# Sparse attention: index weights projected with tokens moving, and the last block's index sum on GpSimd

## What is computed

```python
h = x @ w_in
c_q, c_kv, k_idx, w_idx = jnp.split(h, [Q_LORA, Q_LORA + KV_LORA, Q_LORA + KV_LORA + IDX_DIM], axis=-1)
c_q = rms_norm_2(c_q, q_norm_g)             # 256 wide
c_kv = rms_norm_2(c_kv, kv_norm_g)          # 128 wide, "the latent"
q_idx = (c_q @ w_qidx).reshape(B, S, IDX_HEADS, IDX_DIM)
k_idx = layer_norm(k_idx, kidx_g, kidx_b)
w_idx = w_idx * (IDX_HEADS ** -0.5 * IDX_DIM ** -0.5)   # 8 weights per token
...
    s_idx = jnp.einsum('bthd,bsd->bths', qi_b, k_idx)
    score = jnp.einsum('bths,bth->bts', jax.nn.relu(s_idx), wi_b)
    score = jnp.where(causal[None], score, -jnp.inf)
    _, sel = lax.top_k(score, topk)         # topk = 128
```

## Time and profile before

| | us |
|---|---|
| median of 3 runs | 2138.32 |
| lowest and highest | 2128.67, 2138.58 |
| the profiled execution | 2141.42 |
| its span | 2139.6 |
| busy: TensorE, its weight loads | 2019.0, 1549.9 |
| busy: VectorE, ScalarE, GpSimd | 1269.6, 814.8, 253.0 |

### The profile page before, as it was taken

How to read it: one execution, slowest core, us unless ns; L and a number is a source line. 1 busy time by engine, 2 the same in 40 slices (tenths; PEclk the granted TensorE clock), 3 DMA queues, 4 the chain that set the end, 5 groups by cost and what they waited for, 6 DMA issues and landing times. The chain is left out here.

```text
span 2139.6 us, 31913 instructions
## 1 busy us (share of the span) xinstructions
PE 2019.0 (94%) x13493; PEld 1549.9 (72%) x13493; DVE 1269.6 (59%) x1814; ACT 814.8 (38%) x1222; POOL 253.0 (12%) x175
## 2 busy tenths in 40 slices
PE   7999998999997997889799999999988999999998
PEld 3876776888785872788477888887545678888886
DVE  2335764767546468676557666634388567667535
ACT  3444654344332336322333222322257442222323
POOL 0000002424430001410600000000017200000000
PEclk9998999999998998999999999999999999999999
DMA  7323002212231420000122233232320013322331
GB/s 287 96 88 119 1 1 59 89 50 69 80 97 52 113 78 14 4 4 4 39 79 79 99 98 98 90 99 86 102 73 1 30 52 106 96 93 98 98 98 41
DMA packets 47054, 158.43 MB, mean 74 GB/s; under 512 B 5344, under 2 KB 7520, under 8 KB 46912
## 3 DMA queue, kind: packets, MB, share of 16 engines
q1 hardware_dynamic: 45328, 151.90, 22.4%
q10 hardware_dynamic: 1584, 4.49, 0.7%
HBM read 154.23 MB, written 2.14 MB: 73 GB/s over the span
## 5 line engine op out<-in xcount | busy, mean ns | idle before, releaser
L1043 PE MATMUL banks<-up_x_high,up_w_high 128*128 128x512 f32 x1056 | 412.1, 390 | 6.6 <-DVE up_w_low L1037 3.9
L1044 PE MATMUL banks<-up_x_low,up_w_high 128*128 128x512 f32 x1056 | 411.6, 390 | 0.0
L1045 PE MATMUL banks<-up_x_high,up_w_low 128*128 128x512 f32 x1056 | 411.5, 390 | 0.0
L1037 DVE TENSOR_TENSOR up_w_low<-weight_ring,up_w_high 128x1024 fp32r<-128x1024 f32 x132 | 161.6, 1225 | 269.9 <-ACT up_w_high L1032 269.9
L1032 ACT CAST up_w_high<-weight_ring 128x1024 fp32r<-128x1024 f32 x132 | 138.3, 1049 | 365.2 <-PE banks L1045 340.7
L1043 PEld LDWEIGHTS banks<-up_x_high,up_w_high 128*128 128x128 f32 x1056 | 198.7, 188 | 51.5 <-issue 9.5
L1045 PEld LDWEIGHTS banks<-up_x_high,up_w_low 128*128 128x128 f32 x1056 | 198.7, 188 | 41.6
L1044 PEld LDWEIGHTS banks<-up_x_low,up_w_high 128*128 128x128 f32 x1056 | 198.6, 188 | 40.7
L1579 POOL TENSOR_TENSOR hproj_w_low<-weight_ring,hproj_w_high 128x1024 fp32r<-128x1024 f32 x43 | 106.0, 2467 | 498.7 <-ACT hproj_w_high L1379 498.7
L1098 DVE SCALAR_TENSOR_TENSOR act<-banks,cols,act 128x511 f32<-128x511 f32 (+1 forms) x176 | 131.8, 749 | 6.2
L1254 PE MATMUL banks<-hproj_x_high,hproj_w_high 128*128 128x512 f32 x224 | 90.2, 403 | 5.2 <-DVE hproj_x_low L1530 3.4
(11 more groups left out here) (483 smaller groups left out, 4011.3 us busy)
## 6 DMA issues: line engine op xcount, KB each, us to landing
weight_ring<-in_up SPq DMA_DIRECT2D x88, 512.0 KB, 3.4
weight_ring<-in_down SPq DMA_DIRECT2D x44, 512.0 KB, 3.4
weight_ring<-in_w_ada SPq DMA_DIRECT2D x24, 512.0 KB, 4.7
weight_ring<-in_w_rkv SPq DMA_DIRECT2D x24, 512.0 KB, 3.6
weight_ring<-in_w_in SPq DMA_DIRECT2D x20, 512.0 KB, 3.6
weight_ring<-in_w_out SPq DMA_DIRECT2D x16, 512.0 KB, 3.6
weight_ring<-in_w_q SPq DMA_DIRECT2D x8, 512.0 KB, 4.7
weight_ring<-in_w_k SPq DMA_DIRECT2D x8, 512.0 KB, 3.6
```

The costliest lines, as they stand in the source:

```text
L1037: nc.vector.tensor_tensor(w_low[:, n % 2, :], ring[:, i % RING, :], w_high[:, n % 2, :].bitcast(f32), ALU.subtract).then_inc(wl_made, 1)
L1043: nc.tensor.matmul(PS[:, bank, :], high, x_high[:, k, :], start=start, stop=False)
L1044: nc.tensor.matmul(PS[:, bank, :], high, x_low[:, k, :], start=False, stop=False)
L1045: return nc.tensor.matmul(PS[:, bank, :], low, x_high[:, k, :], start=False, stop=stop)
```

## The change

Three things change, all in the one block. The index weights are projected with x as the moving operand: for each of the eight channel tiles a matmul of 512 tokens whose held operand is 8 useful columns wide, on column group k % 4, so that groups 0 to 3 each hold the sum of two tiles (`PS[:, 5, :]`). ScalarE copies this to SBUF (`w_rows`), and four small matmuls against a 0/1 matrix (`w_picked`, made by VectorE at the block's start) add the four groups and turn the result to tokens by heads. The first step stands ahead of the query sum, the turning behind the index queries. Block 3's index sum goes from VectorE to GpSimd, as a multiply and an add for each head where VectorE has one fused instruction, ahead of GpSimd's five for the latent's root. VectorE's selection of blocks 1 and 2 follows right behind their sums. The number of weight loads and all else stay.

```diff
@@ -2527,6 +2527,9 @@
             sem(n) for n in ("w_idx_taken", "q_idx_taken", "q_taken", "index_scores_made", "index_relu", "index_added", "selected"))
         kv_copied, kv_squared, kv_summed, kv_rooted, kv_fixed, kv_turned = (
             sem("ckv_" + n) for n in ("copied", "squared", "summed", "rooted", "fixed", "reversed"))
+        last_weighted, last_added = sem("last_index_weighted"), sem("last_index_added")
+        w_pick, w_rows_taken, w_turned = sem("w_idx_pick"), sem("w_idx_rows_taken"), sem("w_idx_turned")
+        w_rows, w_halves, w_picked = qd[:, 7, :], small[:, 96:112], small[:, 112:120]
         expanded, expanded_moved = sem("latent_expanded"), sem("latent_expanded_moved")
         first = at["used"]
         QI_BANK = [1, 2, 3, 6]
@@ -2548,6 +2551,11 @@
                 project(0, ln_ready)
                 project(1)
                 project(2)
+                w = next_chunk(pe)
+                for k in range(8):
+                    g, n = k % 4 * 32, min(32, 64 - 8 * k)
+                    mm = nc.tensor.matmul(PS[g:g + n, 5, :], w[:, k * 8:k * 8 + n], x[:, k, :], start=k < 4, stop=k >= 4, skip_group_check=True)
+                mm.then_inc(weight_used, 1)
                 pe.wait_ge(band_taken, 1)
                 for i in range(2):
                     pe.wait_ge(q_squared, i + 1)
@@ -2555,11 +2563,6 @@
                 mm.then_inc(q_summed, 1)
                 pe.wait_ge(d_in_taken, 3)
                 nc.tensor.matmul(PS[:, 7, :], mat("ones"), k_idx, start=True, stop=True).then_inc(k_mean, 1)
-                w = next_chunk(pe)
-                for b in range(NB):
-                    for k in range(8):
-                        mm = nc.tensor.matmul(PS[:, 0, b * 8:(b + 1) * 8], x[:, k, b * P:(b + 1) * P], w[:, k * 8:(k + 1) * 8], start=k == 0, stop=k == 7)
-                mm.then_inc(weight_used, 1)
                 pe.wait_ge(k_squared, 1)
                 nc.tensor.matmul(PS[:, 4, :], mat("ones"), sq_k, start=True, stop=True).then_inc(k_summed, 1)
                 for i in range(4):
@@ -2569,6 +2572,11 @@
                             pe.wait_ge(q_scaled, k + 1)
                         mm = nc.tensor.matmul(PS[:, QI_BANK[i], :], w[:, k * P:(k + 1) * P], low[:, k, :], start=k == 0, stop=k == 1)
                     mm.then_inc(weight_used, 1)
+                pe.wait_ge(w_rows_taken, 1)
+                pe.wait_ge(w_pick, 2)
+                for b in range(NB):
+                    mm = nc.tensor.matmul(PS[:, 0, b * 8:(b + 1) * 8], w_rows[:, b * P:(b + 1) * P], w_picked, start=True, stop=True)
+                mm.then_inc(w_turned, 1)
                 pe.wait_ge(w_idx_taken, 1)
                 pe.wait_ge(k_shifted, 1)
                 pe.wait_ge(qi_taken, 4)
@@ -2618,6 +2626,8 @@
                 act.wait_ge(eps_made, 2)
                 act.wait_ge(q_summed, 1)
                 nc.scalar.activation(root_q, PS[:, 6, :], ACT.Abs_reciprocal_sqrt, bias=eps_q).then_inc(q_rooted, 1)
+                act.wait_ge(weight_used, first + 4)
+                nc.scalar.copy(w_rows, PS[:, 5, :]).then_inc(w_rows_taken, 1)
                 act.wait_ge(k_centred, 1)
                 nc.scalar.activation(sq_k, k_idx, ACT.Square, scale=P ** -0.5).then_inc(k_squared, 1)
                 act.wait_ge(k_summed, 1)
@@ -2659,6 +2669,10 @@
             def _(dve):
                 nc.vector.memset(eps_q, 1e-6).then_inc(eps_made, 1)
                 nc.vector.memset(eps_k, 1e-5).then_inc(eps_made, 1)
+                one_of_four = mat("ident").rearrange("p (g c) -> p g c", c=32)
+                nc.vector.tensor_tensor(w_halves.rearrange("p (g h) -> p g h", h=8), one_of_four[:, 0:2, 0:8], one_of_four[:, 2:4, 0:8], ALU.add).then_inc(w_pick, 1)
+                dve.wait_ge(w_pick, 1)
+                nc.vector.tensor_tensor(w_picked, w_halves[:, 0:8], w_halves[:, 8:16], ALU.add).then_inc(w_pick, 1)
                 ln["vector"](dve)
 
                 def inverse_root(total, eps, root, fix, rooted, fixed):
@@ -2679,12 +2693,12 @@
                 for i in range(2):
                     nc.vector.scalar_tensor_tensor(out=low[:, i, :], in0=low[:, i, :], scalar=col("q_norm_g", i), in1=root_q,
                                                    op0=ALU.mult, op1=ALU.mult).then_inc(q_scaled, 1)
-                dve.wait_ge(weight_used, first + 4)
-                nc.vector.tensor_scalar(w_idx, PS[:, 0, 0:32], 8 ** -0.5 * 64 ** -0.5, None, ALU.mult).then_inc(w_idx_taken, 1)
                 inverse_root(PS[:, 4, :], eps_k, root_k, fix_k, k_rooted, k_fixed)
                 nc.vector.scalar_tensor_tensor(out=k_idx, in0=k_idx, scalar=col("kidx_g", 0), in1=root_k, op0=ALU.mult, op1=ALU.mult).then_inc(k_scaled, 1)
+                dve.wait_ge(w_turned, 1)
+                nc.vector.tensor_scalar(w_idx, PS[:, 0, 0:32], 8 ** -0.5 * 64 ** -0.5, None, ALU.mult).then_inc(w_idx_taken, 1)
                 dve.wait_ge(w_idx_taken, 1)
-                for b in range(1, NB):
+                for b in range(1, LAST):
                     n = (b + 1) * P
                     for i in range(8):
                         dve.wait_ge(sc_relu, 8 * (b - 1) + i + 1)
@@ -2697,7 +2711,7 @@
                                                            op0=ALU.mult, op1=ALU.add).then_inc(sc_added, 1)
                     dve.wait_ge(sc_added, 9 * (b - 1) + 8)
                     nc.vector.tensor_tensor(left(b)[:, b * P:n], left(b)[:, b * P:n], mat("neg_after"), ALU.add).then_inc(sc_added, 1)
-                dve.wait_ge(sc_added, 27)
+                dve.wait_ge(sc_added, 18)
                 for k in range(TOPK // 8):
                     for b in range(1, LAST):
                         if k:
@@ -2715,6 +2729,19 @@
 
             @block.gpsimd
             def _(pool):
+                pool.wait_ge(w_idx_taken, 1)
+                for i in range(8):
+                    pool.wait_ge(sc_relu, 8 * (LAST - 1) + i + 1)
+                    wcol = w_idx[:, LAST * 8 + i:LAST * 8 + i + 1]
+                    weighted = left(LAST) if i == 0 else rel[i]
+                    nc.gpsimd.tensor_scalar(weighted, rel[i], wcol, None, ALU.mult).then_inc(last_weighted, 1)
+                    if i:
+                        pool.wait_ge(last_weighted, i + 1)
+                        if i > 1:
+                            pool.wait_ge(last_added, i - 1)
+                        nc.gpsimd.tensor_tensor(left(LAST), left(LAST), rel[i], ALU.add).then_inc(last_added, 1)
+                pool.wait_ge(last_added, 7)
+                nc.gpsimd.tensor_tensor(left(LAST)[:, LAST * P:T], left(LAST)[:, LAST * P:T], mat("neg_after"), ALU.add).then_inc(last_added, 1)
                 pool.wait_ge(kv_rooted, 2)
                 nc.gpsimd.tensor_tensor(fix_kv, var_kv, root_kv, ALU.mult).then_inc(kv_fixed, 1)
                 pool.wait_ge(kv_fixed, 1)
```

## The result

| | us |
|---|---|
| before, median of 12 runs | 2137.75 |
| changed, median of 12 runs | 2142.28 |
| ratio, 95% interval | 1.0026 (1.0014 to 1.0038) |
| changed, the profiled execution and its span | 2140.54, 2138.7 |

The changed kernel is a quarter of a per cent slower, 4.5 us by the medians. This lies within the 0.5% that the prediction called no change, though the interval doesn't hold 1. The two profiled executions alone would not have told: the page of the changed kernel has a span 0.9 us *shorter* than before.

What follows compares the result with a forecast made beforehand. One block counts: TensorE bounds it up to the index scores, VectorE after. Scores 6.5 us earlier, GpSimd's delayed expansions and 1.8 us of clock put the next block at 1601.3 against 1600.5: +0.8, time 2139.1, range 2128 to 2145.

Steps and rivals of the forecast that it cites:

- The 1.6 us that VectorE's relief can give at most: At the block's end ScalarE finishes only 1.6 us before VectorE, so taking work off VectorE alone gives at most that.
- GpSimd's chain: Block 3's sum, then the latent's root, in GpSimd's in-order queue: root fixed 36.1 us behind the first index score.
- the expansions' start: TensorE's expansions would start 37.5 us behind the first index score, where before it was 30.4.
- The column groups: The index weights' 16 new passes of 512 columns run nearly four abreast on TensorE, 1.9 us; bounds 1.7 to 7.0.
- The clock's fall ahead of the expansions: TensorE idles some 7.8 us there, then runs 3.6 us at half pace: 1.8 us lost, between 0 and 1.8.
- the forecast A: Likeliest case for the whole change: -1.0 to +2.6 us, likeliest +0.8, time 2139.1; chance 0.68.
- the prediction's own signs of being wrong: Among them, at the block's end: next block starting at a distance from the expansions other than 15 to 17 us.
- the clock in the first half: TensorE's two gaps, some 2.7 us, before the query projections: full clock likeliest, up to 1.8 us lost if it fell.
- Rival B: GpSimd's multiplies in block 3's sum take 0.62 us, so the block gains 8.1 us, time 2130.2; chance 0.12.
- Rival C: VectorE's memory reads slow GpSimd during block 3's sum: +2.1 to +10.1 us, 2141.2 to 2149.2; chance 0.14.
- S': Predicted start of the index scores in the changed block: 1547.1 us, 6.5 us earlier than before.
- Rival D: The index weights' column groups run one after another, 7.0 us in place of 1.9, time 2144.2; chance 0.06.

Runs made afterwards that it cites:

- the root between the heads: Changed kernel with GpSimd's five latent-root instructions moved between the fifth and sixth head of block 3's sum; ratio 0.9966, or 0.9971 with TensorE's head gaps also filled.
- the filled head: Changed kernel with one unused 128x512 matmul in each of TensorE's two gaps ahead of the index query projections; ratio 1.0015.
- part 1 alone: Changed kernel with block 3's sum back on VectorE, keeping the index weights projected with tokens moving; ratio 0.9966 to the kernel before.
- with the constant: Changed kernel, GpSimd's eight multiplies by constant 0.5 plus an added 0.0, block 3's index weights left out; no ratio, block 101.8 us against 109.6 before.
- with the column: Changed kernel, GpSimd's eight multiplies by the weights' column given a second operation, an added 0.0; ratio 0.9982 to the kernel before.

## Why the prediction was right or wrong

**Right in kind.** The 1.6 us that VectorE's relief can give at most: Q was 45.3 in both kernels with the root between the heads, against 46.9 and 47.0. GpSimd's chain becomes what is late: the expansions' start was put at 37.5 behind the first score and was 37.7 in every kernel with the change's order. The multiply's price 1.558 against 1.566, the add's 1.27 against 1.269, the sum 22.9 against 23.2 (1551.70 to 1574.86). The column groups: 1.9 against 1.86, so four abreast. The Trainium skill (TensorE: Matmul & The Clock Gate, "Part 3: Packing small matmuls") gives 2.38x for three column tiles; the estimate from it was 2.9 us, and the 1.86 measured for four groups does not follow it. The clock's fall ahead of the expansions: 1.8 against 2.4 and 1.6, and 2.8 with the filled head.

**Not right in size.** Predicted +0.8 us, measured +4.5 by the medians and +3.2 in the traced block. Both lie above +2.6, where the forecast A ended. That the kernels came out as good as equal needed no more than that both halves were small beside 2138 us. One of the prediction's own signs of being wrong showed too: the next block began 17.4 us behind the first expansion (1582.16 to 1599.56), outside its 15 to 17, because the clock cost more there than it was priced at.

**The term that was mis-sized** is the clock in the first half. The step "TensorE does the key sum in between, idling some 2.7 us in two gaps, and starts the query projections" kept the full clock as the likeliest and allowed "up to 1.8 us" for a fall. The gaps were as foreseen (1.45 and 1.20 us, from the trace), but the clock fell in seven of eight profiles, and cost 1.4 to 3.0 us (H 18.0 to 19.7 against 16.6): in the changed kernel's profile it was at half for the first 6 us of the projections, not 3.6. The 3.6 was read from the one row where work after an idle time was dense from its first pass on the earlier trace rows. Put in, the profile's block closes: +0.8 forecast, +2.8 for H (19.7 against the sum's 16.9), +0.9 for Q (55.1 against 54.2, of which 0.6 is the tail's clock beyond 1.8), -1.3 for L make +3.2, and 112.85 - 109.63 is 3.2. The -1.3 is luck; without it the block would have come out 4.5 us longer than before.

**Rival B** (GpSimd quick enough) did not come, and I had rejected it for a wrong reason. I took the row of 0.62 to be quick because its factors are constants. Constants alone take 1.49; the form with two operations is quick with a column too. The rule of the Trainium skill that I set beside it (GPSIMD Engine Reference, "4.1 Engine selection": one-input work roughly at line rate) holds here for two operations, 0.62 to 0.71 us beside 0.48 for VectorE's multiply of the same size by a column (L2693), and not for one, 1.49 to 1.57, three times that. The measurement decides: one-input is no sufficient description.

**Rival C** (GpSimd and VectorE hold each other up) is real but small in the chain that counts, and falls on VectorE too, which I had not asked. The first three of GpSimd's multiplies took 1.94, 1.70 and 1.87 us while VectorE summed block 2, the later ones 1.55 to 1.57, and VectorE's fused instructions there went to at most 1.445 us:

```profile
L2710 DVE SCALAR_TENSOR_TENSOR act<-ffn_act,small,act x14: 483/552/1445, 1546.2 to 1555.7; 128x256 f32<-128x256 f32 x7, 128x384 f32<-128x384 f32 x7
```

Before, the longest of this line's form, on a wider tile, was 0.75 us. The seven fused instructions of block 2's sum, before and in the changed kernel:

```profile
1560.03 4.95 DVE L2696 SCALAR_TENSOR_TENSOR act<-ffn_act,small,act 128x384 f32<-128x384 f32 x7
...
1550.94 6.18 DVE L2710 SCALAR_TENSOR_TENSOR act<-ffn_act,small,act 128x384 f32<-128x384 f32 x7
```

In part 1 alone, where GpSimd has nothing to do at that time, they took 4.95 us again. In the changed kernel block 2's sum with its mask took 7.4 us (1550.42 to 1557.81) instead of 5.8, so VectorE ended at S' + 41.5, not 39.8. Nothing waits for it, so it cost nothing. Beside the selection both ran at full speed. Rival D did not occur: the column groups ran four abreast.

## What to carry to other kernels

Before work is moved to an idle engine, look at what already stands in that engine's queue and who waits for it; the same instructions in an order that lets the awaited ones through were worth 9.8 us of this block (2.4 of it through the clock), and in the bad order multiplies less than half as long were worth 9.4 with the constant and 6.9 with the column. When several engines end nearly together, the distance to the second one is all that relieving the first can give: here 1.7 us, and the change to the index weights, which shortened what they all share, was worth 5.2 us of H, and 6.7 with the gaps filled. Gaps of 1.45 and 1.20 us on TensorE were not free ahead of dense work here: price the clock with the passes behind it, and fill the gap if the price matters.

## What the runs showed that I had not expected

- On GpSimd a tensor-by-scalar instruction of 128x512 float32 with one operation took 1.49 us (constant) or 1.57 (column), and with a second operation, an added zero, 0.66 or 0.71. Why is open.
- TensorE's clock fell to half behind idle gaps of 1.45 and 1.20 us with 1.1 us of work between them in seven profiles of eight, and with one matmul of two passes in each gap it stayed at 1.00 (four of four).
- 16 passes of 512 columns over four column groups took 1.86 us, 3.7 times less than 16 x 0.43 one after another.
- GpSimd's multiplies and VectorE's fused instructions with two inputs were both longer side by side: up to 1.94 for 1.57 us, and up to 1.45 for at most 0.75. Beside VectorE's selection GpSimd's were not. What they share that does it was not tried.
- Medians of the very same kernel before, taken beside different experiments, were 2136.57 to 2139.25, and single runs 2124.7 to 2145.9: differences of 2 us between kernels are seen in the block's trace and not in the times. Where that scatter comes from outside this block is open.
